# One hybrid encoder layer on one Trainium2 core: branch A's gate products spread over the attention and among 32x32 products, with a new order of the projections and of the last expert pair

## The reference, cut to what matters

```
proj = h @ w_in                                   # D -> q | k | v | rwkv features | branch gates
att  = windowed_attention(q, k, v, sink) @ w_br_attn      # blocks of 128 queries, 2 or 3 key blocks, 8 heads
rw   = rwkv7_bidir(feat, ...) @ w_br_rwkv                 # forward and backward scan over 512 tokens
g_att, g_rw = split(sigmoid(gl), 2)
x = x + gt1 * ((g_att * att + g_rw * rw) @ w_out)
h = rmsnorm(x, norm2_g) * (1 + sc2) + sh2
x = x + gt2 * expert_choice_moe(h, router_w, w_gate, w_up, w_down)   # 16 experts, 64 tokens each
return rmsnorm(x, final_g)
```

## Time and profile before

| what | value |
|---|---|
| runs | 1619.11, 1620.9, 1621.21 us |
| the profiled execution's own time | 1617.86 us |
| its span, first to last instruction | 1616.1 us |
| busy: TensorE matmul, weight load | 1403.0 us (87%), 674.8 us (42%) |
| busy: VectorE, ScalarE, GpSimd | 473.0 us (29%), 205.1 us (13%), 42.6 us (3%) |
| mean granted TensorE clock | 0.958 |
| chain that ended last | TensorE 58%, DMA 29%, VectorE 7%, issue 3% |

### The profile page before, as it was taken

How to read it: one execution, slowest core, us unless ns; L and a number is a source line. 1 busy time by engine, 2 the same in 40 slices (tenths; PEclk the granted TensorE clock), 3 DMA queues, 4 the chain that set the end, 5 groups by cost and what they waited for, 6 DMA issues and landing times.

```text
span 1616.1 us, 21549 instructions
## 1 busy us (share of the span) xinstructions
PE 1403.0 (87%) x9239; PEld 674.8 (42%) x9239; DVE 473.0 (29%) x806; ACT 205.1 (13%) x394; POOL 42.6 (3%) x45
## 2 busy tenths in 40 slices
PE   4996999899768999599979989989989989889886
PEld 2442454444667445335325325334343343243332
DVE  2899826632226431510210210210200200201103
ACT  2023011111222201111001001001001001010001
POOL 2003400000000000000000000000000000000000
PEclk9997999999799999799999999999999999999998
DMA  9941333331400452799999999999999999999994
GB/s 337 379 168 53 78 79 104 130 78 59 162 33 6 180 187 94 286 417 427 428 429 429 428 429 428 428 428 428 429 429 429 428 428 428 429 429 429 428 428 187
DMA packets 90979, 485.52 MB, mean 300 GB/s; under 512 B 36043, under 2 KB 53533, under 8 KB 62373
## 3 DMA queue, kind: packets, MB, share of 16 engines
q1 hardware_dynamic: 90576, 484.30, 73.6%
q10 hardware_dynamic: 341, 0.30, 0.1%
HBM read 470.93 MB, written 10.50 MB: 298 GB/s over the span
## 4 chain that ended last, share of the span: by engine, by line
PE 58%; DMA 29%; DVE 7%; issue 3%; SPq 1%; ACT 1%; ACTq 0%; DVEq 0%
PE psum L1061 14%; DMA arena<-in_exp_w_up_dram 13%; DMA arena<-in_exp_w_gate_dram 12%; PE psum L1076 10%; PE psum L661 7%; PE psum L554 4%; PE psum L1042 4%; PE psum L948 3%; PE psum L977 3%; DMA arena<-in_ada_w_dram 3%; PE psum L1120 2%; SPq L263 1%; PE psum L700 1%; DVE arena L1394 1%; PE psum L753 1%
## 5 line engine op out<-in xcount | busy, mean ns | idle before, releaser
L1061 PE MATMUL psum<-arena 128*64 128x512 f32 x2048 | 471.2, 617 | 83.9 <-DMA arena<-in_exp_w_up_dram 63.6
L1061 PEld LDWEIGHTS psum<-arena 128*64 128x64 f32 x2048 | 164.8, 142 | 383.4 <-issue 383.0
L1076 PE MATMUL psum<-arena 128*64 128x512 f32 x1024 | 224.6, 596 | 13.1 <-issue 11.4
L554 PE MATMUL psum<-arena 128*128 128x512 f32 x336 | 147.1, 599 | 9.1 <-DVE arena L1429 9.1
L1076 PEld LDWEIGHTS psum<-arena 128*64 128x64 f32 x1024 | 86.2, 138 | 145.9 <-issue 145.8
L661 PE MATMUL psum<-arena 128*128 128x512 f32 x256 | 123.6, 613 | 0.0
L554 PEld LDWEIGHTS psum<-arena 128*128 128x128 f32 x336 | 64.3, 192 | 91.3 <-issue 90.5
L1788 DVE TENSOR_TENSOR arena<-arena,psum 128x512 f32<-128x512 f32 x32 | 19.8, 682 | 268.3 <-PE psum L1061 268.3
L1790 DVE TENSOR_TENSOR arena<-psum,arena 128x1024 f32<-128x1024 f32 x8 | 9.8, 1225 | 288.7 <-PE psum L1076 288.7
L1780 DVE TENSOR_TENSOR arena<-arena,psum 128x512 f32<-128x512 f32 x32 | 19.8, 682 | 171.0 <-ACT arena L1339 171.0
L1794 DVE TENSOR_TENSOR arena<-arena,psum 128x512 f32<-128x512 f32 x64 | 44.0, 688 | 83.2 <-PE psum L1120 83.2
(11 more groups left out here) (262 smaller groups left out, 1078.9 us busy)
## 6 DMA issues: line engine op xcount, KB each, us to landing
arena<-in_exp_w_gate_dram SPq DMA_DIRECT2D x64, 2048.0 KB, 24.6
arena<-in_exp_w_up_dram SPq DMA_DIRECT2D x64, 2048.0 KB, 26.7
arena<-in_exp_w_down_dram SPq DMA_DIRECT2D x64, 2048.0 KB, 27.0
arena<-in_ada_w_dram SPq DMA_DIRECT2D x24, 1024.0 KB, 10.1
arena<-in_w_in_dram SPq DMA_DIRECT2D x16, 1024.0 KB, 5.8
arena<-in_x_dram SPq DMA_DIRECT2D x2, 2048.0 KB, 8.8
gate_pre<-arena SPq DMA_DIRECT2D x16, 256.0 KB, 5.8
arena<-in_w_out_dram SPq DMA_DIRECT2D x1, 4096.0 KB, 20.7
```

The lines of the kernel that those rows point to most:

```text
L554: ins = mm(bank(b % 4), by(w_ring[g % 2], KC)[:, k, j * P:(j + 1) * P], by(hT, KC)[:, k, :], start=(k == 0), stop=(k == KC - 1))
L1061: ins = mm(bank(4 * kind + n)[e * 64:(e + 1) * 64, :], by(xeT, KC)[:, k, e * 64:(e + 1) * 64], by(ring[(j + e) % RING], 2)[:, r, n * 512:( ...
L1076: ins = mm(bank(4 + n)[e * 64:(e + 1) * 64, :], by(hidT, FBLK)[:, 4 * kk + b, e * 64:(e + 1) * 64], by(ring[(j + e) % RING], 4)[:, b, n * ...
```

## The change

1. *Start.* SP issues five of the ten parameter loads ahead of `x`, ScalarE the other five; the four `ada_b` loads go behind the eighth `ada_w` piece, with a semaphore of their own that only VectorE waits for. The last transpose of `x` moves into the first projection.
2. *Projections.* The k, v and q blocks come as b = 7 to 12, the last eight feature blocks as b = 13 to 20. `kk_raw` moves into VectorE's decay sums, behind m = 2. The eight late shifts move behind `beta_ready`. The bonus products move behind the A products, and v's transposes to where the late blocks are.
3. *Attention.* Each query block has 26 gate products: 8 between the scores, 6 behind the last scores, 8 in the heads, 4 at the end. The block of 32 is gone. The 30 steps of the inverse go two by two behind the probability copies of query blocks 1 and 2.
4. *32x32 products.* They are cut into pieces, with 24 gate products among them. VectorE and ScalarE share the copies.
5. *Branches.* The last two attention branch blocks are made later, and the output projection waits for each k by itself.
6. *Last expert pair.* The last down pieces are loaded in halves, the result is scaled and put back by halves, and the final norm squares by halves.

```diff
-GROUPS = [FEAT_COL + 12 * P, FEAT_COL + 14 * P] + [FEAT_COL + f * P for f in (4, 6, 8, 10, 0, 2)] + [HEADS * HD, 0, 2]
+GROUPS = [FEAT_COL + 12 * P, FEAT_COL + 14 * P] + [FEAT_COL + f * P for f in (4, 6)] + [HEADS * HD, 0, 2]
+GROUPS += [FEAT_COL + f * P for f in (8, 10, 0, 2)]
+EARLY, ATT_BLOCKS = 7, 6
...
-            pe.wait_ge(sem("params_in"), 224)
+            pe.wait_ge(sem("params_in"), 160)
...
-            for b in range(7, 11):
+            for b in range(7, 9):
                 project(b)
             pe.wait_ge(sem("lora_out"), 19)
             pe.wait_ge(sem("kk_sq"), 1)
...
-            for b in range(11, 15):
+            for b in range(9, 12):
                 project(b)
...
+            for b in range(12, 18):
+                project(b)
+            pe.wait_ge(sem("att_copy"), 2)
+            pe.wait_ge(sem("kk_normed"), 1)
...
+            pe.wait_ge(sem("kk_normed"), 4)
+            pe.wait_ge(sem("shift_done"), 11)
...
-            for b in range(15, 21):
+            for b in range(18, 21):
                 project(b)
...
+            pe.wait_ge(sem("kk_raw"), 1)
+            pe.wait_ge(sem("bonus_in"), 1)
+            for m in range(PAIRS):
+                pe.wait_ge(sem("A_made"), 5 + m)
+                mm(bank(4 + m), head_rk[:, m * P:(m + 1) * P], by(bon, PAIRS)[:, m, :], start=True, stop=True) \
+                    .then_inc(sem("bonus_mm"), 1)
...
-                g0 = (0, 56, 80, 104)[q]
+                g0 = 26 * q
...
+                gate_products(g0 + 8, g0 + 14)
...
-                    gate_products(g0 + 8 + h, g0 + 9 + h)
+                    gate_products(g0 + 14 + h, g0 + 15 + h)
...
-                gate_products(g0 + 16, g0 + 24)
+                gate_products(g0 + 22, g0 + 26)
...
-                if q == 0:
-                    gate_products(24, 56)
...
+            pe.wait_ge(sem("T_in"), 12 * 16)
+            for n in range(2):
+                x_blocks(0, 16 * n, 16 * n + 16)
+                gate_products(104 + 2 * n, 106 + 2 * n)
+            pe.wait_ge(sem("attT_ready"), TT)
+            for n in range(2):
+                x_blocks(1, 16 * n, 16 * n + 16)
+                gate_products(108 + 2 * n, 110 + 2 * n)
+            pe.wait_ge(sem("pool_prep"), 1)
+            for d in range(DIRS):
+                C(0, d)
+            gate_products(112, 116)
+            pe.wait_ge(sem("X_out"), 4)
+            for d in range(DIRS):
+                for n in range(3):
+                    t_blocks(d, (0, 11, 22)[n], (11, 22, 32)[n])
+                    gate_products(116 + 6 * d + 2 * n, 118 + 6 * d + 2 * n)
+            pe.wait_ge(sem("gate_raw"), GATEB)
...
             pe.wait_ge(sem("wo_in"), 16)
-            pe.wait_ge(sem("mixT_ready"), KC)
...
                 for k in range(KC):
+                    if t + n == 0:
+                        pe.wait_ge(sem("mixT_ready"), k + 1)
...
+                if m == 2:
+                    dve.wait_ge(sem("lora_mm"), 20)
+                    for k in range(PAIRS):
+                        s(v.tensor_scalar(by(KKt, 4)[:, k, :], by(Kt, 4)[:, k, :], pcol[:, KKC + k:KKC + k + 1], None,
+                                          ALU.mult))
+                        s(v.tensor_scalar(head_rk[:, k * P:(k + 1) * P], head_ones, pcol[:, RKC + k:RKC + k + 1], None,
+                                          ALU.mult))
+                    dve.sem_inc(sem("kk_raw"), 1)
...
-            for b in range(7, 11):
-                shift(b)
...
-            for b in range(11, 15):
-                shift(b)
...
             dve.sem_inc(sem("beta_ready"), 1)
...
+            for n in range(EARLY, FB):
+                shift(n)
...
+            def last_narrow(i):
...
+                        for b in (2 * half, 2 * half + 1):
+                            for e in range(2):
+                                ins = mm(bank(4 + n)[e * 64:(e + 1) * 64, :],
+                                         by(hidT, FBLK)[:, 12 + b, e * 64:(e + 1) * 64],
+                                         by(ring[6 + e], 4)[:, b, n * 512:(n + 1) * 512], start=False, stop=(b == 3))
...
+                if last:
+                    last_narrow(i)
+                    pe.wait_ge(sem("put_ready"), i + 1)
+                    for n in range(2):
+                        pe.wait_ge(sem("ye_ready"), i + 1 + n)
+                        for t in range(TT):
+                            mm(bank((6, 0, 1, 2, 3, 4, 5, 7)[n * TT + t]), put[:, t * P:(t + 1) * P],
+                               ye[:, n * 512:(n + 1) * 512], start=True, stop=True).then_inc(sem("put_mm"), 1)
+                    return
...
                     v.tensor_copy(pT[n % 2][:, 0:w], bank(4 + n % 2)[:, 0:w]).then_inc(sem("pT_ready"), 1)
+                    if q in (1, 2):
+                        if (q, h) == (1, 0):
+                            dve.wait_ge(sem("tri_in"), 16)
+                        for i in range(16 * q + 2 * h - 15, 16 * q + 2 * h - 13):
+                            if i < HALF - 1:
+                                invert(i)
```

More of the change, by code:

```diff
@@ L289, in _ @@
                 ada_piece(n)
+            for q in range(4):
+                load(adab_first[quarter(q), :], ada_b[0:1, 512 * q:512 * (q + 1)].partition_broadcast(32), "first_in")
             weights(0)
@@ L1106, in pair @@
                     ins.then_inc(sem("hidT_mm"), 1)
-                for kk in range(4):
+                for kk in range(3):
                     narrow(i, kk)
+                if not last:
+                    narrow(i, 3)
+                else:
+                    pe.wait_ge(sem("hidT_ready"), 4 * i + 4)
                 pe.wait_ge(sem("pick_aff_ready"), i + 1)
```

276 lines of the change are left out of this document (151 added, 125 removed).

## The result

Four runs of the changed kernel gave 1592.18, 1594.55, 1597.66 and 1598.0 us, median 1596.1; four of the kernel before, on the same chip, 1620.4. The ratio is 0.9848 (95% interval 0.9826 to 0.987). The profiled execution took 1594.55 us with a span of 1592.7, against 1617.86 and 1616.1: 23.4 us less. The forecast was 16.7 us less, 1604 us. Its range of 1594 to 1612 holds the median; its inner band, 1598 to 1610, which had a chance of 0.58, does not.

A forecast was written before the change was run, and what follows sets the result against it. Expert weight transfers were taken as a fixed block, its end moved by the stages before: 0 + 1.7 + 25.7 - 16.5 + 1.5 + 2.3 + 2.0 = 16.7 us off, from 1617.86 to 1601.2; median forecast 1604, range 1594 to 1612.

The forecast's parts named there:

- The start: Up to about 100 us: earlier first products against a later x, VectorE's modulation setting the time; 0, 2 us either way.
- The projections: From b = 7 to the second pair of scores: 3.2 us earlier, less 1.5 us of slow clock; 1.7 us gained.
- The attention: Query blocks: 32 products, exponential waits and slow clock removed, less added products and slower heads; 25.7 us shorter.
- the heads: Attention blocks 1 and 2: VectorE's inverse steps pace seven heads, 19.5 us against 12.7; 13.5 us lost, kept 8 to 18.
- The 32x32 section: End of attention to first B products, with 24 gate products mixed in: 36.6 us where it was 20.1, 16.5 longer.
- rival A: 32x32 products: clock stays at 1.2 GHz, section 39.7 us longer; kernel 8 us slower, 1629; chance 0.07.
- The scan: First scan products behind the 32x32 section: the clock stays up, so they gain 1.5 us.
- Branches and end: Wait for the last mix before the output projection goes, 2.3 us; puts of the last pair start 2.0 us earlier.
- The expert part: From about 670 us: DMA engines full with weights, a block of fixed length that the diff does not shorten.
- rival C: The inverse costs less (heads lose 5 instead of 13.5) or the clock pays back more: 1595; chance 0.15.
- B: The middle loses: kk_sq late, L1477's copy blocked by GpSimd, longer pool_prep wait; 4 to 8 us less, 1610; chance 0.15.
- D: Heads of blocks 1 and 2: TensorE's pauses bring the clock down, some 11.7 us more over 14 heads, 1616; chance 0.05.

The follow-up runs named there:

- e3: Changed kernel with 28 of the inverse's 30 steps left out (only i = 1 and 2 computed): 1584.5 us, ratio 0.9763 to the kernel before.
- e2: Changed kernel with the six gate products behind each query block's last scores moved to the block's end: 1613.6 us, ratio 0.9941 to the kernel before.
- e5: Changed kernel with two more blocks (b = 9, 10) ahead of the sums of squares, norms' spread behind b = 13: 1588.6 us, ratio 0.981 to before.
- e10: Changed kernel without VectorE's GpSimd wait before the first logits, two more blocks ahead of the sums of squares, inverse steps spread singly: 1574.7 us, 0.9713 to before.
- e8: The changed kernel run again without any edit: 1593.6 us, ratio 0.9842 to the kernel before.
- the execution called after: The profiled execution of the changed kernel, without further edits: 1594.55 us, against 1617.86 for the kernel before.
- e11: As e10, with GpSimd's first two multiplies waiting for beta and v's transposes ahead of b = 17: 1566.7 us, ratio 0.9663 to the kernel before.

## Why the prediction was right, and where it was off

- **The start, 0.** Right, 0.25 us: VectorE's work on `ada_w` sets the time at 100 us. To a quarter of a microsecond it is luck: over the executions of the change and its variants b = 7 stands at 98.4 to 101.7 us.
- **The projections, 1.7.** 3.4 us at the second pair of scores; the slow clock that the forecast took off there lies behind it (block 0 took 30.17 us, 28.57 without it), so the net is 1.8. The wait was 11.03 us for 11.5, the logits 234.50 for 234.7. beta was ready at 173.6 and not at 179, which nothing waited for. The terms listed up to the end of b = 20 add up to 218.1, not 218.4; it ended at 218.0.
- **The attention, 25.7.** With the 1.6 us of block 0 counted apart it is 30.4. The term that was mis-sized is the heads: 13.5 forecast, 10.7 measured (e3). VectorE's seven heads of a block took 18.1 us (its copies stand at 282.10 and 300.18), where I had put 19.5. The slow clock paid back 6.2 us where 4.7 was put: blocks 1 to 3 of before, less their waits and plus the two products, are 2.15, 1.75 and 2.3 us longer than those of e3. The waits (13.2, e2) and the 32 products stand. Each of these sizes is read from one or two executions.
- **The 32x32 section, -16.5.** -15.1. The clock was 1.00, which decided against rival A. The section measured 35.3 us where 36.6 was put; the half of the 2.4 us of idle issue that I kept did not come.
- **The scan, 1.5.** 1.1: the clock's gain at its start was partly spent in the slow stretch at 420 to 431 us, longer than the one in the kernel before (clock 0.81 and 0.77 from 440 to 448).
- **Branches and end, 2.3 and 2.0.** 2.5 at the output projection, 2.1 at the puts.
- **The expert part** kept its length to 0.7 us, which no term had.

Sum of the misses: 0.3 + 0.1 + 4.7 (of which 2.8 heads, 1.5 clock) + 1.4 - 0.4 + 0.2 + 0.7 - 0.2 = 6.8 us, against 6.7 measured. The mechanisms were right. Nearly every miss lies on the same side, and the median is in the range because the range took in rival C. Of the 8 us between forecast and median 6.7 are these misses; the rest is that the median stood 3.0 us above the profiled execution before and 1.6 us after.

Of the rivals, C (the inverse costs less, or the clock pays back more) is the nearest: both halves of it came true in part, and the profiled execution, 1594.55, is where it stood. B did not come as a loss: `kk_sq` came in time and E by r took the short price. One of its conditions was there: the copy that B names, L1477, took 4.57 us beside GpSimd's L488 before and 5.44 us after, and a second instruction was held with it. TensorE waited for nothing behind them until e5 and e10, where it waited 3.94 us. D had a chance of 0.05 and is partly true: the clock does fall in the heads, at a cost of 1.7 to 3.2 us in five of eight executions, and in none of the four without the pauses, but the price is far from 11.7 us. (Those 11.7 follow from the mean head of 2.79 us, 19.5 over 7, and not from the 3.2 that stands beside them.) That it is the pauses is the likely reading of five in eight against none in four, not more. Its counter-argument, that the scan pauses as often at 1.00, does not carry over from one pattern to another. The section of the Trainium skill that I set aside there (TensorE: Matmul & The Clock Gate, A second HAM failure mode: psum-queue depth-cycling) says that short pauses between groups of matmuls can lower the clock; the heads of block 1 agree in e8 (0.54 from 300 to 304 us), and not in the execution called after (1.00). This is one of the things by which runs of one kernel differ, and not the largest: e8's execution, with the slow heads, was 2.3 us faster than that called after.

The Trainium skill (SBUF — State Buffer, SBUF: two separate sides) names, beside instructions with two SBUF inputs, those in VectorE's two-port mode as excluding GpSimd. The rows of e10 and e11 agree in that instructions with one source can be held: a maximum with a constant, one source in SBUF, takes 4.78 us beside GpSimd and 0.43 without it. No row names an instruction's mode, and the reciprocal between the two held ones, one source as well, kept its 3.35 us. I had applied only the first half of the rule.

The 0.89 given for a faster kernel is low by its own parts: the forecast, B and C alone make 0.88, and most of D's 0.05 comes on top.

## What to carry to other kernels

Work that is handed to an engine with room in its pauses should be cut to the size of each pause and spread over all of them: 30 steps two by two in two blocks cost 10.7 us, one by one over three blocks less than 0.1 in each. Small products that would run at the lower clock can be mixed with large ones that have to be made anyway, and the pauses that a reordering leaves should be priced with the clock behind them. When a wait has been moved, look at the next engine in the chain: GpSimd, at work at the same time, held a 0.43 us instruction of VectorE for 4.78. And before a gain is read off two traces, look at what was not edited: here the start alone moved by over 2 us and a block by 1.6 or 3 between executions.

## What the runs showed that I had not expected

- The clock's falls are not the same in every execution of one kernel: block 0 of the attention took 28.57 or 30.17 us, block 1 40.05 or 43.0 to 43.3 (once 41.74), with the same pauses.
- With loads under way while TensorE runs short instructions, a pause without a releaser is 3.7 to 4.5 us; in the one execution without them it was 1.8.
- A copy of 128x32 elements took 5.44 us on VectorE beside a GpSimd multiply (0.13 alone), while a reciprocal at the same time kept its 3.35 us.
